# Input projection of the second feed-forward in seven products of quarters instead of eight

## The reference, cut to what matters

```
def swiglu(h, w_in, w_out):
    gate, up = jnp.split(h @ w_in, 2, axis=-1)
    return (jax.nn.silu(gate) * up) @ w_out
...
x = x + g2 * swiglu(modulate(rms_norm(x, norm_gain[i, 1]), sh2, sc2), ffn_w_in[i], ffn_w_out[i])
```

## Time and profile before

| | |
|---|---|
| median of 3 runs | 2438.05 us (2434.53 to 2441.36) |
| span of the profiled execution | 2437.8 us |
| TensorE busy | 2374.0 us, 97% |
| VectorE, ScalarE, GpSimd busy | 54%, 36%, 15% |
| DMA | 220.77 MB, mean 91 GB/s |
| first feed-forward | about 154 to 690 us |
| second feed-forward | about 1125 to 1490 us |

### The profile page before, as it was taken

One profiled execution on the slowest core, in us unless ns is written; L12 is line 12 of the kernel. 1 busy time (PEld: TensorE's weight loads), 2 busy tenths in 40 slices (PEclk: granted clock), 3 DMA queues, 4 the chain that ended last, 5 costly groups with the idle time before them and its releaser, 6 DMA issues.

```text
span 2437.8 us, 34490 instructions
## 1 busy us (share of the span) xinstructions
PE 2374.0 (97%) x14220; PEld 1983.3 (81%) x14220; DVE 1317.2 (54%) x2149; ACT 879.4 (36%) x1499; POOL 374.9 (15%) x301
## 2 busy tenths in 40 slices
PE   7899999999999999999999999999999999999999
PEld 6678888888887777656888887988989878887788
DVE  3775635643546776785333336375566445555433
ACT  4332111211134444444212224454445334445432
POOL 0210000000015444501000001143343410000000
PEclk9999999999999999999999999999999999999999
DMA  9834334334321111112233333212222122112223
GB/s 323 210 101 124 121 117 125 121 121 121 108 79 36 39 52 35 35 49 71 88 104 91 99 87 104 70 52 70 70 70 68 55 73 67 53 58 65 87 87 113
DMA packets 252743, 220.77 MB, mean 91 GB/s; under 512 B 7480, under 2 KB 243443, under 8 KB 252204
## 3 DMA queue, kind: packets, MB, share of 16 engines
q1 hardware_dynamic: 249072, 217.92, 29.3%
q10 hardware_dynamic: 3260, 0.58, 0.1%
q0 software_dynamic: 256, 0.07, 0.0%
HBM read 214.26 MB, written 6.29 MB: 90 GB/s over the span
## 4 chain that ended last, share of the span: by engine, by line
PE 60%; DVE 3%; ACT 2%; issue 1%; POOL 1%; DMA 1%; SPq 0%; DVEq 0%; ACTq 0%; POOLq 0%
PE two L689 11%; PE bank L1547 5%; PE bank L1356 5%; PE bank L689 4%; PE bank L1352 3%; PE bank L1333 3%; PE two L1287 3%; PE bank L1053 2%; PE bank L1528 2%; PE two L1158 2%; PE two L1567 2%; PE bank L1184 2%; PE bank L1023 1%; PE bank L1035 1%; PE two L1445 1%
## 5 line engine op out<-in xcount | busy, mean ns | idle before, releaser
L2578 DVE TENSOR_TENSOR wL<-ring,wH 128x512 fp32r<-128x512 f32 x224 | 179.5, 817 | 144.4 <-ACT wH L1842 144.3
L1833 ACT ACTIVATE wH<-ring 128x2048 fp32r<-128x2048 f32 (+1 forms) x80 | 149.2, 1865 | 265.4 <-PE bank L694 71.6
L2567 DVE TENSOR_TENSOR wL<-ring,wH 128x2048 fp32r<-128x2048 f32 (+1 forms) x80 | 179.8, 2247 | 79.5 <-ACT wH L1833 79.3
L689 PE MATMUL two<-h1H,wH 128*128 128x512 f32 x496 | 195.0, 393 | 0.0
L689 PE MATMUL two<-h1H,wL 128*128 128x512 f32 x496 | 193.1, 389 | 0.0
L689 PE MATMUL two<-h1L,wH 128*128 128x512 f32 x496 | 193.0, 389 | 0.0
L1842 ACT ACTIVATE wH<-ring 128x512 fp32r<-128x512 f32 x224 | 133.7, 623 | 57.6 <-PE bank L1333 20.5
L1912 ACT ACTIVATE gateS<-two 128x512 f32<-128x512 f32 x44 | 26.3, 598 | 320.5 <-PE bank L694 136.8
L2671 DVE SCALAR_TENSOR_TENSOR xT<-two,ada,xT 128x512 f32<-128x512 f32 (+1 forms) x48 | 30.6, 680 | 176.4 <-PE bank L694 62.5
L1356 PE MATMUL bank<-unH,wH 128*128 128x272 f32 (+1 forms) x368 | 111.2, 302 | 3.9 <-ACT cin L2103 2.2
L689 PEld LDWEIGHTS two<-h1H,wH 128*128 128x128 f32 x496 | 93.1, 188 | 20.2 <-issue 2.1
(11 more groups left out here) (650 smaller groups left out, 6938.9 us busy)
## 6 DMA issues: line engine op xcount, KB each, us to landing
ring<-in_ffn_w_in SPq DMA_DIRECT2D x88, 512.0 KB, 5.2
ring<-in_w_in SPq DMA_DIRECT2D x40, 1024.0 KB, 5.2
ring<-in_w_ada SPq DMA_DIRECT2D x32, 1024.0 KB, 5.2
ring<-in_ffn_w_out SPq DMA_DIRECT2D x16, 1024.0 KB, 5.2
early<-in_w_ada SPq DMA_DIRECT2D x12, 1024.0 KB, 12.1
ring<-in_diff_w_in SPq DMA_DIRECT2D x12, 1024.0 KB, 5.1
ring<-in_w_proj_ssd SPq DMA_DIRECT2D x8, 1024.0 KB, 5.1
ring<-in_ffn_w_out SPq DMA_DIRECT2D x8, 768.0 KB, 4.7
```

The costliest lines, as they stand in the source:

```text
L689: m = nc.tensor.matmul(bank[3 * s + half], w, r[:, 0:LAT], start=i == 0, stop=i == n - 1)
L1833: nc.scalar.activation(hi, raw, ACT.Copy).then_inc(w_hi, 1)
L2567: nc.vector.tensor_tensor(lo, raw, hi.bitcast(F32), ALU.subtract).then_inc(w_lo, 1)
L2578: nc.vector.tensor_tensor(lo, raw, hi.bitcast(F32), ALU.subtract).then_inc(q_lo, 1)
```

## The change

The input projection of units 1 to 21 of the second feed-forward is computed as a 2 x 2 block product with seven multiplications. The quarters are: the activations by half of the features (512) and half of the rows (256), the weights by half of the features and by gate and up. A product is then 4 chunks of features x 3 parts = 12 matmuls of 256 columns; there are seven per unit (`seven_products`), which accumulate in three banks. Four of the seven left operands are mixtures of activation quarters, made once at the start (`mixtures` on VectorE, `mixed_hi` on ScalarE); for them the modulated activations are kept unsplit (`hraw`), and GpSimd adds the shift to them.

Four of the seven right operands are sums of weight quarters. They are made for all columns beforehand in DRAM (`wsums0` to `wsums3`, 512 x 2816 each): GpSimd issues 16 copies (`weight_sums`), waits for them, issues eight transfers that add to their destination, waits, four more, waits, four more. They stand in its queue between the squares of norm 1 and those of norm 2. Each is 128 rows of 11264 bytes, cut into two runs of 5632.

A unit's weights are seven parts of 256 KB (128 x 512 per partition) instead of one block of 1 MB: four in one ring slot ("in"), three in the other ("ib"). Each part is transferred, split and freed by itself. SyncE waits for all sums before the first part of unit 1. The evacuations change with it: between the products ScalarE copies banks out and VectorE adds, 256 columns at a time (`beside_products`), and a bank is accumulated on after its copy.

```diff
+PARTED = [(kind, 1, c) for c in range(1, FC) for kind in ("in", "ib")]
+PART_OF = {key: 7 * (key[2] - 1) + (0 if key[0] == "in" else 4) for key in PARTED}
+PARTS = {"in": (("g", 0), ("g", 4), (1,), (0,)), "ib": ((2,), (3,), ("u", 4))}
...
+                if unit in PARTED:
+                    plan += [("ib",) + unit[1:]]
...
+    wsums = [nc.dram_tensor(f"wsums{i}", (KC // 2 * P, F), F32).ap() for i in range(4)]
...
+                    if key == PARTED[0]:
+                        sp.wait_ge(*after(w_added, 32 * 16))
+                    for i, which in enumerate(PARTS[key[0]]):
+                        if PLAN[before] in PARTED:
+                            sp.wait_ge(*after(part_lo, PART_OF[PLAN[before]] + i + 1))
+                        elif i == 0:
+                            sp.wait_ge(*blocks_used(PLAN[before]))
+                        if len(which) == 1:
+                            w = wsums[which[0]][:, P * key[2]:P * key[2] + P]
+                        else:
+                            half, kc = which
+                            w = io["ffn_w_in"][1][P * kc:P * kc + 4 * P, (F if half == "u" else 0) + P * key[2]:(F if half == "u" else 0) + P * key[2] + P]
+                        sp.dma_start(part(slot(n), i).rearrange("p (c n) -> p c n", c=4), w.rearrange("(c p) n -> p c n", p=P)) \
+                            .then_inc(part_in[first + i][0], 16)
+                    return
...
+            def seven_products(c):
+
+                key = ("in", 1, c)
+                s = begin(key)
+                q, n = PART_OF[key], LAT // 2
+                a, b, d = bank[3 * s][:, 0:n], bank[3 * s + 1][:, 0:n], bank[3 * s + 2][:, 0:n]
+                whole, low = slice(0, 4), slice(4, 8)
+                products = ((a, h3, whole, 0, 0), (d, h3, low, 0, 0), (a, mixes, 1, 1, 1), (b, mixes, 0, 2, 0),
+                            (a, mixes, 2, 3, 2), (b, h3, low, n, 3), (a, mixes, 3, 4, 4))
+                for i, (to, x, at, mix, kept) in enumerate(products):
+                    n_block = S_OF[("in" if i < 4 else "ib", 1, c)]
+                    w = [part(t[:, n_block % NS], i % 4) for t in (wH, wL)]
+                    pe.wait_ge(*after(part_lo, q + i + 1))
+                    if x is mixes:
+                        if c == 1:
+                            pe.wait_ge(*after(mix_lo, mix))
+                        x = [t[:, at] for t in mixes]
+                    else:
+                        x = [t[:, at, mix:mix + n] for t in h3]
+                    if i in (2, 4, 5, 6):
+                        pe.wait_ge(*after(part_kept, 4 * (c - 1) + (2 if i == 4 else 3 if i == 5 else 4 if i == 6 else 1)))
+                    for k in range(12):
+                        kc, y, z = k // 3, *((0, 0), (0, 1), (1, 0))[k % 3]
+                        m = nc.tensor.matmul(to, w[y][:, P * kc:P * kc + P], x[z][:, kc, :], start=k == 0 and i in (0, 1, 3), stop=k == 11,
+                                             skip_group_check=True)
+                        if k == 0 and i >= 5:
+                            m.then_inc(tile_done, 1)
+                    m.then_inc(part_done[0], 1)
...
+            def beside_products(k):
+
+                s, c, n, half = T_OF[("in", 1, k)] % 2, FC + k, S_OF[("in", 1, k)], LAT // 2
+                q = PART_OF[("in", 1, k)]
+                x, g = bank[3 * s][:, 0:half], gate3[:, c % 2]
+
+                def next_hi(i):
+                    m, r = (n + NS, i) if i < 4 else (n + 1 + NS, i - 4)
+                    if SPLIT[m] in PARTED:
+                        if r < len(PARTS[SPLIT[m][0]]):
+                            part_split_hi(m, r)
+                    elif i in (3, 6):
+                        split_hi(m)
+
+                for i in range(7):
+                    if i == 0 and k > 1:
+                        kept_first(k)
+                    if i == 2:
+                        act.wait_ge(*after(part_done, q + 3))
+                        nc.scalar.activation(g[:, half:LAT], x, ACT.Copy).then_inc(part_kept[0], 1)
+                    if i == 3:
+                        act.wait_ge(*after(part_done, q + 4))
+                        act.wait_ge(g_full, c)
+                        nc.scalar.activation(turns[:, 0], bank[3 * s + 1][:, 0:half], ACT.Copy, scale=-1.0).then_inc(part_kept[0], 1)
+                    if i == 4:
+                        act.wait_ge(*after(part_done, q + 5))
+                        nc.scalar.activation(turns[:, 1], x, ACT.Copy, scale=-1.0).then_inc(part_kept[0], 1)
+                    if i == 6:
+                        act.wait_ge(*after(g_sum, 2 * k))
+                        nc.scalar.activation(g, g, ACT.Silu).then_inc(g_silu, 1)
+                    next_hi(i)
+                    if i == 3 and k == 1:
+                        mixed_hi(3, 4)
+
+            def kept_first(k):
+
+                act.wait_ge(g_hid, FC + k - 1)
+                act.wait_ge(*after(part_done, PART_OF[("in", 1, k)] + 1))
+                nc.scalar.activation(gate3[:, (FC + k) % 2, 0:LAT // 2], bank[3 * (T_OF[("in", 1, k)] % 2)][:, 0:LAT // 2], ACT.Copy).then_inc(part_kept[0], 1)
...
+            def mixtures():
+
+                half = LAT // 2
+                b11, b12, b21, b22 = (hraw[i][:, :, half * j:half * j + half] for i in range(2) for j in range(2))
+                dve.wait_ge(*after(mix_raw, KC))
+                nc.vector.tensor_tensor(b11, b11, b12, ALU.subtract).then_inc(mix_made[0], 1)
+                dve.wait_ge(*after(mix_made, 1))
+                nc.vector.tensor_tensor(b12, b22, b12, ALU.subtract).then_inc(mix_made[0], 1)
+                dve.wait_ge(*after(mix_made, 2))
+                nc.vector.scalar_tensor_tensor(out=b22, in0=b11, scalar=-1.0, in1=b22, op0=ALU.mult, op1=ALU.subtract).then_inc(mix_made[0], 1)
+                dve.wait_ge(*after(mix_made, 3))
+                first_hidden()
+                for i, (at, x) in enumerate(((1, b22), (0, b11), (2, b12))):
+                    dve.wait_ge(*after(mix_hi, i + 1))
+                    nc.vector.tensor_tensor(mixes[1][:, at], x, mixes[0][:, at].bitcast(F32), ALU.subtract).then_inc(mix_lo[0], 1)
+                part_split_lo(S_OF[("ib", 1, 1)], 0)
+                nc.vector.scalar_tensor_tensor(out=b21, in0=b22, scalar=-1.0, in1=b21, op0=ALU.mult, op1=ALU.subtract).then_inc(mix_made[0], 1)
+                for r in (1, 2):
+                    part_split_lo(S_OF[("ib", 1, 1)], r)
+                dve.wait_ge(g_hi, FC + 1)
+                nc.vector.tensor_tensor(hid3[1][:, 0], gate3[:, FC % 2], hid3[0][:, 0].bitcast(F32), ALU.subtract).then_inc(g_hid, 1)
+                dve.wait_ge(*after(mix_hi, 4))
+                nc.vector.tensor_tensor(mixes[1][:, 3], b21, mixes[0][:, 3].bitcast(F32), ALU.subtract).then_inc(mix_lo[0], 1)
...
+                for i in range(7):
+                    if i == 2:
+                        dve.wait_ge(*after(part_kept, 4 * (k - 1) + 1))
+                        dve.wait_ge(*after(part_done, q + 2))
+                        nc.vector.tensor_tensor(g[:, 0:half], g[:, 0:half], bank[3 * s + 2][:, 0:half], ALU.add).then_inc(g_sum[0], 1)
+                    if i == 5:
+                        dve.wait_ge(*after(part_kept, 4 * k))
+                        link(nc.vector.tensor_tensor(turns[:, 1], turns[:, 0], turns[:, 1], ALU.add))
+                        dve.wait_ge(*after(part_done, q + 6))
+                        nc.vector.tensor_tensor(g[:, half:LAT], g[:, half:LAT], bank[3 * s + 1][:, 0:half], ALU.add).then_inc(g_sum[0], 1)
+                    if i == 6:
+                        dve.wait_ge(*after(part_done, q + 7))
+                        dve.wait_ge(g_silu, c + 1)
+                        link(nc.vector.scalar_tensor_tensor(out=g[:, 0:half], in0=bank[3 * s][:, 0:half], scalar=-1.0, in1=g[:, 0:half],
+                                                            op0=ALU.mult, op1=ALU.mult))
+                        dve.wait_ge(v_chain, link.n - 1)
+                        nc.vector.tensor_tensor(g[:, half:LAT], g[:, half:LAT], turns[:, 1], ALU.mult).then_inc(g_full, 1)
+                    next_lo(i)
...
+            def weight_sums():
+
+                w = io["ffn_w_in"][1]
+                g0, g1, u0, u1 = (w[4 * P * i:4 * P * i + 4 * P, F * j:F * j + F] for j in range(2) for i in range(2))
+
+                def quarters(to, src, op=ALU.bypass):
+                    for r in range(4):
+                        pool.dma_start(to[P * r:P * r + P], src[P * r:P * r + P], accum_op=op, max_dma_last_dim=2 * F).then_inc(w_added[0], 16)
+
+                quarters(wsums[0], u0)
+                quarters(wsums[2], g0)
+                quarters(wsums[1], g0)
+                quarters(wsums[3], g1)
+                pool.wait_ge(*after(w_added, 16 * 16))
+                quarters(wsums[0], u1, ALU.add)
+                quarters(wsums[2], u0, ALU.add)
+                pool.wait_ge(*after(w_added, 24 * 16))
+                quarters(wsums[1], wsums[0], ALU.add)
```

(10 more changed lines are left out.)

144 lines of the change are left out of this document (122 added, 22 removed).

## The result

The changed kernel takes 2544.24 us (median; 2542.18 to 2546.76) against 2437.34 us: 1.0431 times, 95% interval 1.0416 to 1.0446. Slower was forecast, but 2474 us, and the range ended at 2530.

What follows compares the result with a forecast made beforehand. TensorE, busy 97% of the span, was taken as the bound. The terms summed as 2438.0 - 21.4 (units) + 10.5 (start) + 6.2 (group ends) + 40.3 (sums in memory) = 2473.6, said as 2474 us; range 2427 to 2530.

Steps and rivals of the forecast that it cites:

- What leaves TensorE: Second feed-forward: 21 units go from 10.89 to 9.87 us each with 256-column matmuls at 117.5 ns, saving 21.4 us.
- The engines' own work beside a steady unit: Second feed-forward: ScalarE's 7.1 us and VectorE's 7.6 us per unit fit under 9.87 us, so no wait.
- The start: Second feed-forward, units 1 and 2: late activation mixtures and the VectorE backlog cost 10.5 us, bounds 5 and 14.
- The group ends: Last unit before each of three down projections: two whole blocks split between evacuations cost 6.2 us, bounds 2 and 9.
- The sums in memory: First feed-forward: GpSimd's long runs delay the weight stream, three waits of 3.1, 18.4 and 18.8 us, 40.3 us in all.
- The same steps with 442: First feed-forward waits with an adding run at 442 ns, two reads not overlapping: 3.1 + 46.6 + 46.6 = 96 us.
- block 3: First feed-forward weight block, issued at 178.56 after 156 of 256 copy runs, landing at 204.6, causing 3.1 us of wait.
- Case B: Stream not held up, GpSimd's queue too slow or several stream runs per turn: 2433 us, no visible change; chance 0.19.
- C: Stream not held up, and smaller waits in the second feed-forward: 2424 us, faster; chance 0.22.
- D: Stream unhindered, but copies and adds miss product 2 in every unit of the second feed-forward: 2454 us; chance 0.06.
- the rule of whole packets: Skill's rule: an engine drains 9 to 17 descriptors per ring; the stream would keep half the engines' time, losing nothing.
- the signs: If right: TensorE idle some 40 us in three pieces between 200 and 340 us, landings two to six times 5.2 us.

## Why the prediction was wrong

The direction, the place and the mechanism were right; the step that failed is the price of the sums in memory, 40.3 us where the runs show 93.1 of waits and 8.7 behind them. In the prediction's own steps:

- What leaves TensorE: -16.9 in place of -21.4. I took 117.5 ns for a 256-column matmul from tiles that follow a 512-column tile. Seven products in a row go at 120.0 ns. Between 226.9 ns for 512 columns and 120.0 for 256 lie 0.418 ns a column; that leaves about 13 ns in either that don't depend on the columns (an estimate from these two paces), against 8 with the 117.5. Why the first feed-forward's is quicker stays open.
- The engines' own work beside a steady unit: right. No wait in a unit, the weights of 186 GB/s hidden.
- The start: 10.5 forecast, 12.2 measured. The sum is near, two parts in it weren't: GpSimd's addition (1.85 us, not 1.2), and that VectorE's low part is longer beside it, which lengthened unit 0.
- The group ends: 6.2 forecast, 5.1 measured.
- The sums in memory: this step failed. "A queue gets a turn per run, whatever its length" is what the runs show. But I took 221 ns for an adding run, the low end of my two, as "the row's own rate", and it takes 440. The same steps with 442 gave 96 us; the waits are 93.1. That these two agree so well is partly luck, since the copying run was too low as well, 262 ns in the mean for 221: when block 3 was issued at 177.51, 123 of an engine's 256 copying runs had passed and not 156, so it met them to its end and landed at 218.80, after 41 us and not 26. The first wait was 18.7 us and not 3.1, and the later ones were shorter than the steps with 442 had them. And I gave these waits no price beyond their length: each of the four left TensorE some 2.2 us behind at the lower clock, 8.7 in all.
- The range: its upper end was the 2529 that the 442 ns gave, with none of these smaller terms of the same sign on top: 8.7 of clock, 4.5 in the units, 1.7 at the start, and 1.8 around the span where the prediction had 0.2. An end that is itself a full estimate needs its own margin.
- Case B (several stream runs per turn, or a slow GpSimd) and with it C are excluded by the equal counts; D didn't occur. What the prediction drew from the rule of whole packets was wrong besides: if both queues' packets held equally many runs, taking whole packets in turn would give the stream no more runs than one and one does, so it would not have kept "half the engines' time". Only the spacing of the single runs tells the two apart.

Of the signs, three pieces of idle time totalling 40 us were four totalling 93, from 204.7 to 356 us; the first ended with a short copy that stood behind the low part of its block on VectorE's queue, the others with a low part, as said; the landings were up to eleven times 5.2 us and not two to six; waits ended before 400 us, as said.

## What to carry to other kernels

In this case transfers on another queue were priced by turns, not by bytes: while one of their runs was always pending, each run of the critical stream waited for one of theirs. So either such runs are made as short as the stream's (13 us left here), or, better, they are issued a few at a time, paced by the consumer's progress, so that the stream finds the engines free most of the time (nothing measurable left here). An engine with nothing to do until much later has all the time for such pacing, and its waits cost nothing. And where a range's end comes from an unmeasured price, take that price as likely unless a row speaks against it.

## What the runs showed of the hardware

- Adding runs take 440, 129 and 65 ns for 5632, 1408 and 512 bytes, DRAM to DRAM; copying runs of 5632 bytes 215 in the median and 262 to 275 in the mean beside the stream.
- One packet of each of the two queues in turn, with runs of 5632 and of 1408 bytes (1474 to 1473, 3176 to 3174, 1638 to 1638 for copies).
- A limit of 512 or 1408 bytes held for adding transfers, while copying ones moved runs of 4096 and 4224 bytes in the records.
- Beside GpSimd's additions VectorE's low part takes 1.18 us in place of 0.75, and its other operation there 0.75 as before; beside ScalarE's additions both take 0.75.
